# Splitting the four prompt tiles and the sample of a hybrid layer into three passes over the weights instead of two

## The reference

```python
h = x + token_mixer(rmsnorm(x))     # w_in 1024 x 3080, width-3 and width-4 causal convs, SSD scan, w_out
h = h + cross_attn(rmsnorm(h))      # w_mq, 4 heads over 256 memory tokens, w_mo
h = h + peer(rmsnorm(h))            # w_pq; 8 heads x top 16 of 128 x 128 product keys
# peer, per token: 8 x 16 experts e with gates g
#   out = sum_e g_e * gelu(x . u_tab[e]) * v_tab[e]     (16384 experts, u and v rows of 1024)
```

## Time and profile before

| what | us |
|---|---|
| median of 3 runs | 1919.24 |
| lowest, highest | 1911.52, 1919.64 |
| the profiled execution | 1920.86 |
| its span | 1918.8 |
| TensorE busy, of the span | 1707.1 |
| VectorE busy | 1245.2 |
| ScalarE busy | 371.5 |
| GpSimd busy | 734.2 |

### The profile page before, as it was taken

One profiled execution on the slowest core, in us unless ns is written; L12 is line 12 of the kernel. 1 busy time (PEld: TensorE's weight loads), 2 busy tenths in 40 slices (PEclk: granted clock), 3 DMA queues, 4 the chain that ended last, 5 costly groups with the idle time before them and its releaser, 6 DMA issues. The chain is left out here.

```text
span 1918.8 us, 19965 instructions
## 1 busy us (share of the span) xinstructions
PE 1707.1 (89%) x7088; PEld 1263.9 (66%) x7088; DVE 1245.2 (65%) x2560; ACT 371.5 (19%) x914; POOL 734.2 (38%) x597
## 2 busy tenths in 40 slices
PE   6998999989659998988686999999999999999854
PEld 5887788868546776877574666666666666666321
DVE  1252211798679767998996999676555555555773
ACT  2032023102421235523452001101000000000001
POOL 0000000223024437513774555455554555545650
PEclk9999999999769998999888999999999999999977
DMA  5533433768138959967999999999999999999992
GB/s 161 182 117 110 154 110 110 262 219 308 33 121 294 342 163 341 339 221 287 336 415 377 380 394 400 398 356 399 401 399 399 389 400 398 397 390 393 405 350 88
DMA packets 238301, 563.10 MB, mean 293 GB/s; under 512 B 17068, under 2 KB 125276, under 8 KB 236156
## 3 DMA queue, kind: packets, MB, share of 16 engines
q0 software_dynamic: 82944, 302.03, 41.6%
q1 hardware_dynamic: 152956, 243.04, 35.7%
...
...
## 5 line engine op out<-in xcount | busy, mean ns | idle before, releaser
L750 POOL DMA_INDIRECT M<-in_u_tab,IDX x288 | 366.6, 1273 | 797.1 <-DVE PEER L1675 408.3
L1064 PE MATMUL PSB<-M,HST 128*128 128x512 f32 x1024 | 466.2, 601 | 51.6 <-DVE HST L1754 49.7
L757 POOL DMA_INDIRECT M<-in_v_tab,IDX x288 | 364.0, 1264 | 340.7 <-DVE X L1696 252.0
L1056 PE MATMUL PSB<-XN,M 128*128 128x256 f32 x2048 | 467.6, 382 | 6.9 <-DMA M<-in_u_blocks 5.9
L1056 PEld LDWEIGHTS PSB<-XN,M 128*128 128x128 f32 x2048 | 391.4, 192 | 105.9 <-issue 56.6
L1064 PEld LDWEIGHTS PSB<-M,HST 128*128 128x128 f32 x1024 | 196.5, 193 | 259.5 <-issue 247.0
L1675 DVE CUSTOM_DVE_ANT_0 M<-M,XN 128x1024 f32<-128x1024 f32 x288 | 350.4, 1220 | 17.8 <-DMA M<-in_u_tab,IDX 17.2
L799 PE MATMUL PSB<-M 128*128 128x256 f32 (+1 forms) x1408 | 337.8, 402 | 11.9 <-DVE M L1345 10.6
L1696 DVE SCALAR_TENSOR_TENSOR X<-M,PEER,X 128x1024 f32<-128x1024 f32 x256 | 328.0, 1281 | 5.8 <-DMA M<-in_v_tab,IDX 3.3
L799 PEld LDWEIGHTS PSB<-M 128*128 128x128 f32 x1408 | 273.3, 196 | 70.0 <-DVE M L1345 11.5
L806 PE MATMUL PSB<-M 128*128 128x256 f32 (+1 forms) x1056 | 241.9, 389 | 0.0
(11 more groups left out here) (208 smaller groups left out, 1030.9 us busy)
## 6 DMA issues: line engine op xcount, KB each, us to landing
M<-in_u_blocks SPq DMA_DIRECT2D x128, 512.0 KB
M<-in_v_tab SPq DMA_DIRECT2D x128, 512.0 KB
M<-in_w_in SPq DMA_DIRECT2D x24, 1024.0 KB
M<-in_w_pq SPq DMA_DIRECT2D x16, 1024.0 KB
gate_spill<-M ACTq DMA_DIRECT2D x16, 1024.0 KB
M<-gate_spill SPq DMA_DIRECT2D x16, 1024.0 KB
M<-in_w_out SPq DMA_DIRECT2D x8, 1024.0 KB
M<-in_w_mq SPq DMA_DIRECT2D x8, 1024.0 KB
```

Source lines behind the costliest of these rows:

```text
L750: pool.indirect_dma_start(out=UA[:, s % RR, :], out_offset=None, in_=utab, in_offset=bass.IndirectOffsetOnAxis(ap=IDX[:, n:n + 1], axis=0) ...
L757: pool.indirect_dma_start(out=VA[:, s % RR, :], out_offset=None, in_=vtab, in_offset=bass.IndirectOffsetOnAxis(ap=IDX[:, n:n + 1], axis=0) ...
L1056: last = pe.matmul(PSB[:, 4 + b % 2, 0:2 * P], UBLK[:, b % SR, c, :], XN[:, 1:3, c * P:(c + 1) * P], start=(c == 0), stop=(c == DC - 1))
L1064: last = pe.matmul(PSB[:, 2 * t + hf, :], WR[:, b % WRING, t * P:(t + 1) * P], VBLK[:, b % SR, hf * 512:(hf + 1) * 512], start=(b == 0), s ...
```

## The change

The tiles are split into three groups: tile 0, tiles 1 and 2, and tile 3 with the sample. dense(g) is called for each, with 128, 256 and 160 tokens. The memory's kv jobs all stand in the SSD of tile 0, by KV_A to KV_C. Group 1 reads K and V back for itself, group 2 reads them again with the cache's. SP loads the 32 blocks of weights a third time. The histories of the convolutions are kept from group 0 to 1 and from 1 to 2. The planner takes costs by group for in, q and pq (pe_us). It runs in two parts. Over the rest of group 0 and group 1 the extras are the routing of tile 0 and the sparse steps. Over group 2 they are the routings of tiles 1 and 2 (hot[0]) and their one-hot batches (hot[1]), with a number of sparse steps among them: SLOT_SHARE makes it a third of the count of the others (oh and gb counted half). What is left over follows with an lk behind every six (LK_EVERY), up to 19 lk; then the others, and 12 sparse steps (BEFORE_W) ahead of the loop. tt 2 is now a job like tt 1. Scores of tile 2 lie in the buffer of the one-hots, so the first oh of each tile waits until tile 2 is routed. Before the loop SP loads the first u and v blocks in the order in which the last weight buffers come free. Left out below: the same replacement of 256 by the group's width and of group 1 by the last group in the single helpers, the wait counts of K and V by group, and the buffers' sizes.

```diff
@@ -42,9 +42,11 @@
-TG = [[0, 1], [2, 3, 4]]
-ORDER = TG[0] + TG[1]
-NG = [2 * P, 2 * P + SAM]
+TG = [[0], [1, 2], [3, 4]]
+LAST = len(TG) - 1
+ORDER = TG[0] + TG[1] + TG[2]
+WG = [P, 2 * P, P]
+NG = [P, 2 * P, P + SAM]
 DENSE = [1, 2]
@@ -53,11 +55,14 @@
 def group(t):
-    return int(t in TG[1])
+    return [t in tiles for tiles in TG].index(True)
 def pos(t):
     return ORDER.index(t)
+
+
+KV_A, KV_B, KV_C = 3, 7, 11
@@ -84,7 +89,7 @@
     else:
-        s += [("turn", 0, t) for t in TG[1]]
+        s += [("turn", 0, t) for t in TG[g]]
     for b in ("gc", "v", "gb", "x0"):
@@ -94,15 +99,14 @@
     for c in range(3, 8):
-        n = int(g == 0 or c < 5)
-        s += z[:n] + [("cs", g, c)]
-        z = z[n:]
+        s += z[:int(c < 5)] + [("cs", g, c)]
+        z = z[int(c < 5):]
+    between = z
     if g == 0:
-        s += z
         between = [("kv", kv, q, mt) for kv in range(2) for q in range(4) for mt in range(2)]
-        s += soft_chain(TG[0], [between[2 * k:2 * k + 2] for k in range(8)])
-    else:
-        s += soft_chain(TG[1], [[], z[0:1], z[1:2], [], [], z[2:3], z[3:4], [], [], [], [], []]) + [("oc",)]
+    s += soft_chain(TG[g], [between[:KV_A], between[KV_A:KV_B], between[KV_B:KV_C], between[KV_C:]] if g == 0 else [[], z[0:1], z[1:2], [], [], [], [], []])
+    if g == LAST:
+        s += [("oc",)]
     s += [("o", g, q, t) for q in range(4) for t in TG[g]]
@@ -110,24 +114,21 @@
     s += [("q", g, m) for m in range(4)]
-    s += [("kt", 1, st, q) for st in range(2 * g) for q in range(4)]
+    s += [("kt", g, st, q) for st in range(g) for q in range(4)]
     s += [("q", g, m) for m in range(4, 8)]
     for i, t in enumerate(TG[g]):
         s += [("a1", t)] + ([("a2", TG[g][i - 1])] if i else [])
     s += [("a2", TG[g][-1])]
     s += [("mo", g, q, t) for q in range(4) for t in TG[g]]
     s += [("norm", 2, t) for t in TG[g]] + [("sk", g, q) for q in range(4)] + [("turn", 2, t) for t in TG[g]]
-    s += [("keep_x", DENSE[g])]
-    if g == 0:
-        s += [("norm", 0, t) for t in TG[1]]
-    early = TG[1] if g else [0]
+    s += [("keep_x", t) for t in TG[g] if t in DENSE]
+    if g < LAST:
+        s += [("norm", 0, t) for t in TG[g + 1]]
     for m in range(16):
         s += [("pq", g, m)]
         if m % 4 == 0 and m:
-            s += [("sc", t, m // 4 - 1) for t in early]
-    s += [("sc", t, 3) for t in early]
-    if g == 0:
-        s += [("sc", 1, b) for b in range(4)]
+            s += [("sc", t, m // 4 - 1) for t in TG[g]]
+    s += [("sc", t, 3) for t in TG[g]]
     return s
@@ -135,9 +136,15 @@
           "a1": 3.8, "norm": 1.2, "keep": 0.3, "rt": 1.9, "smd": 0.8, "tt": 0.6, "oh": 1.25, "d": 1.3, "v": 1.3, "final": 1.3, "add": 22.0}
-EARLY_STEPS = 5
-G0_STEPS = 2
+SLOT_SHARE = 3
+LK_EVERY, AFTER, BEFORE_W = 6, 5, 12
 LONG = ("in", "z", "o", "q", "mo", "pq")
+
+
+def pe_us(x):
+    if x[0] in ("in", "q", "pq"):
+        return (2.2, 3.9, 2.7)[x[1]]
+    return PE_US.get(x[0], 0.0)
@@ -182,7 +189,7 @@
     lead = work.index(("sc", 0, 0)) + 1
-    out, work = work[:lead], work[lead:] + dense(1)
+    out, work = work[:lead], [work[lead:] + dense(1), dense(2)]
@@ -192,57 +199,54 @@
     slots += [("add", GSTEPS - 1)]
-    step = lambda i: slots.index(("d", i, 0))
-    one, early, mid, last = step(1), step(3), step(EARLY_STEPS), step(EARLY_STEPS + G0_STEPS)
     first = [x for h in range(PH) for x in rt(0, h)] + soft(0)
-    second = [x for h in range(PH) for x in rt(1, h)] + soft(1)
-    extra = first[:4] + merged(first[4:], slots[:one]) + merged(second, slots[one:early])
-    extra += [("tt", 1)] + merged(batches(1), slots[early:mid])
-    late_slots, slots = slots[mid:last], slots[last:]
+    one = slots.index(("d", 1, 0))
+    extra = first[:4] + merged(first[4:], slots[:one]) + slots[one:]
+    hot = [x for t in DENSE for h in range(PH) for x in rt(t, h)]
+    hot = [hot[:4 * PH] + soft(1) + hot[4 * PH:] + soft(2), batches(1) + batches(2)]
     t_pe = t_dve = 0.0
-    gone, held, late, odd = set(out), [], [], 0
-    for w in work:
-        if w[0] in LONG:
-            out += held
-            t_pe += sum(PE_US["gb"] for x in held if x[0] == "gb")
-            held = []
-        while (extra or late) and w[0] in LONG and t_dve < t_pe:
-            odd += 1
-            if late and (odd % 2 or not extra):
-                out.append(late.pop(0))
-                t_dve += dve_us(out[-1])
-                continue
-            if not extra:
-                break
-            x = extra[0]
-            if x[0] == "rt" and ("sc", x[1], x[2] // 2) not in gone:
-                break
-            if x[0] == "oh" and held:
-                break
-            extra.pop(0)
-            if x[0] in ("gb", "tt"):
-                held.append(x)
-                if x[0] == "tt":
+    gone, held = set(out), []
+    for part in range(2):
+        if part == 1:
+            n_slots = (len(hot[0]) + len(hot[1]) // 2) // SLOT_SHARE
+            n_first = n_slots * len(hot[0]) // (len(hot[0]) + len(hot[1]) // 2)
+            later = extra[n_slots:]
+            extra = merged(hot[0], extra[:n_first]) + [("tt", 1), ("tt", 2)] + merged(hot[1], extra[n_first:n_slots])
+        for w in work[part]:
+            if w[0] in LONG:
+                out += held
+                t_pe += sum(PE_US["gb"] for x in held if x[0] == "gb")
+                held = []
+            while extra and w[0] in LONG and t_dve < t_pe:
+                x = extra[0]
+                if x[0] == "rt" and ("sc", x[1], x[2] // 2) not in gone:
                     break
-                continue
-            out.append(x)
-            t_dve += dve_us(x)
-        out.append(w)
-        gone.add(w)
-        t_pe += PE_US.get(w[0], 0.0)
-        t_dve = max(t_dve, t_pe - 10) + dve_us(w)
-        if w[0] == "sc" and w[1] == NP and w[2] < 3:
-            late += rt(2, 2 * w[2]) + rt(2, 2 * w[2] + 1)
+                if x[0] in ("oh", "tt") and held:
+                    break
+                extra.pop(0)
+                if x[0] in ("gb", "tt"):
+                    held.append(x)
+                    continue
+                out.append(x)
+                t_dve += dve_us(x)
+            out.append(w)
+            gone.add(w)
+            t_pe += pe_us(w)
+            t_dve = max(t_dve, t_pe - 10) + dve_us(w)
     out += held
     ahead = [("lk", b) for b in range(HRING)]
-    out += merged(merged(late, extra), ahead[:4]) + merged(rt(2, 6) + rt(2, 7), ahead[4:8]) + ahead[8:9] + soft(2)
-    out += ahead[9:10] + late_slots[:3] + [("tt", 2)]
-    g0, n = [], P // OH_TOK
-    for k in range(0, n, 2):
-        g0 += [("oh", 2, k), ("oh", 2, k + 1)] + ahead[10 + k * 13 // n:10 + (k + 2) * 13 // n] + [("gb", 2, k), ("gb", 2, k + 1)]
-    g0 += ahead[23:]
-    out += merged(g0, late_slots[3:])
+    n = len(extra) // (HRING - AFTER)
+    k = 0
+    for n, x in enumerate(extra):
+        while k < min(HRING - AFTER, n // LK_EVERY):
+            out.append(ahead[k])
+            k += 1
+        out.append(x)
+    out += ahead[k:]
+    slots = later
+    out += slots[:BEFORE_W]
+    slots = slots[BEFORE_W:]
@@ -538,11 +542,12 @@
-            first = (slice(0, 256), slice(hist, hist + 256))
-            if g == 0:
+            w = WG[g]
+            first = (slice(0, w), slice(hist, hist + w))
+            if g < LAST:
                 return [first]
-            s0 = 256 + {0: 2, 2: 4, 3: 6}[hist]
-            return [first, (slice(256, 256 + SAM), slice(s0, s0 + SAM))]
+            s0 = w + {0: 2, 2: 4, 3: 6}[hist]
+            return [first, (slice(w, w + SAM), slice(s0, s0 + SAM))]
@@ -619,6 +624,13 @@
                 if i == BLOCK_AT[("w_mq", 2 * BW, 1)]:
+                    wait_job(sp, ("o", 1, 3, TG[1][-1]))
+                    sp.wait_ge(outs, 16 * 2)
+                    sp.dma_start(KB[0], o["mk"].rearrange("l b (t p) h d -> p (l b t) (h d)", p=P)).then_inc(kb_in, 16)
+                if i == BLOCK_AT[("w_mo", BW, 1)]:
+                    wait_job(sp, ("kt", 1, 0, 3))
+                    sp.dma_start(VV[:, 0], o["mv"].rearrange("l b (t p) h d -> p (l b t) (h d)", p=P)).then_inc(vv_in, 16)
+                if i == BLOCK_AT[("w_mq", 2 * BW, LAST)]:
@@ -674,15 +686,11 @@
                 sp.dma_start(XN[q * SAM:(q + 1) * SAM, NP, :], XN[0:SAM, NP, :]).then_inc(relaid_x, 16)
-            wait_job(sp, BLOCKS[-3][2])
-            u_block(0)
-            u_block(1)
-            wait_job(sp, BLOCKS[-2][2])
-            u_block(2)
-            v_block(0)
-            wait_job(sp, BLOCKS[-1][2])
-            v_block(1)
-            v_block(2)
+            last_of = {i % NW: BLOCKS[i][2] for i in range(len(BLOCKS) - NW, len(BLOCKS))}
+            for r in sorted(range(NW), key=lambda r: SEQN[last_of[r]]):
+                wait_job(sp, last_of[r])
+                for k in (2 * r, 2 * r + 1):
+                    (u_block if k < SR else v_block)(k % SR)
             wait_drained(sp, ("sc", NP, 3))
@@ -1727,10 +1721,9 @@
```

(7 more changed lines are left out.)

114 lines of the change are left out of this document (50 added, 64 removed).

## The result

The kernel got slower: 2041.59 us (median of 4 runs, 2035.63 to 2046.04) against 1917.3 for the kernel before in the same comparison, a ratio of 1.0651 [1.0613, 1.0689], or +124 us. The direction was forecast, the size (+36) was not, and the range (to 1992) doesn't hold it. The profiled execution has a span of 2033.9 us, 115 more than before, with TensorE busy 1746.7 us (1707.1 before).

The account below looks back on a forecast made before the run. It took TensorE's queue as what everything follows before the block loop, with TensorE and DMA full in the loop. Terms 9 + 7 + 15 + 50 - 50 + 5 = +36 us gave 1955 us; range 1908 to 1992.

Parts of the forecast that it names:

- The third pass itself: Dense part: +9 us of TensorE work, +7 for weights read a third time, +50 of gaps nothing covers (30 to 70).
- the 4 us that I gave four of them: Dense part: four gb fewer under it, 20 instead of 24, give 4 us back.
- The term for the weights: Tile 0's pass: weight loads arriving late for three buffers cost 6 to 30 us over 32 blocks, taken as +7.
- its forecast: Sign for tile 0's pass: its dense work ends near 266 us.
- my 7.1 from the earlier trace: Weight loads in tile 0's pass: a 1 MB load takes 7.1 us to land beside other traffic, as K's did.
- my estimate of 4.4 us: Weight loads: by the skill page, 2.0 us plus bytes by 436 GB/s, 4.4 us and no miss.
- The steps in the pair's pass: Pair's pq: gathers make DMA the bound, 26 us over TensorE, softened by rings to 10; +15 us (0 to 30).
- The gain: Stretch behind the dense part: 139 of 185 us remain, so -50 (-65 if nothing waits, -35 if as now).
- The loop: Expert-block loop: 201 sparse steps ahead of it for 208, seven more gathers in it, +5 us (up to 9).
- My "at 1.3 us" a step: Expert-block loop: each of seven more gathers in a stretch full of DMA costs 1.3 us.
- The rivals: Whole kernel: faster, 1895 to 1910, chance 0.14; nothing to see, 1910 to 1929, 0.16; data as bound, 1980 to 2014, 0.15.
- The data-bound one: Rival: the stream of data bounds, both DMA terms at upper ends, +93 us, 1980 to 2014; chance 0.15.

Follow-up runs that it names:

- Experiment 11: Kernel before (two groups) with no sparse step ahead of the loop, all 208 in it: 2119.38 us, ratio 1.1064 to the kernel before.
- experiment 8: Changed kernel with no sparse step up to the end of the pair's pass, 54 ahead of the loop: 2157.21 us, ratio 1.1250 to the kernel before.
- experiment 3: Changed kernel with the gelu of sparse step 4 and three steps behind it moved from the pair's pass to the third: 2037.24 us, ratio 1.0600.
- experiment 4: Changed kernel loading only an eighth of each w_mq and w_pq block in the pair's pass: 2022.74 us, ratio 1.0536 to the kernel before.
- experiment 1: Changed kernel with SP's first three gate reads issued behind the u block of lk 23, not ahead of lk 20's: 2021.63 us, ratio 1.0517.
- experiment 2: Changed kernel with lk among the batches only between oh and gb, not behind every sixth extra: 2009.63 us, ratio 1.0461 to the kernel before.
- experiment 5: Changed kernel with gate reads behind lk 23's u block and lk only between oh and gb: 1986.93 us, ratio 1.0353 to the kernel before.
- 7: Changed kernel, planner reckoning 1.8 us instead of 1.3 per d or v up to the pair's end, 161 steps ahead of the loop: 2064.26 us, ratio 1.0767.
- experiment 10: Changed kernel with the edits of experiment 5 and 34 more extras in the slots, 235 steps ahead of the loop: 1978.12 us, ratio 1.0324.
- after: The changed kernel with three groups, no further edit: 2041.59 us, ratio 1.0651 to the kernel before.
- experiment 9: Changed kernel with the edits of experiment 5, 1.8 us per step up to the pair's end, and 41 steps put among the third group's extras: 1950.42 us, 1.0197.
- experiment 6: Kernel before with five lk instead of one behind the last gb and SP's gate reads behind lk 23's u block: 1917.32 us, ratio 0.9999.

## Why the prediction was right in sign and wrong in size

**The third pass itself (9 + 7 of weights + 50 of gaps): right in its sum.** Experiment 11 has no step in the dense part and experiment 8 none up to the pair's end, so they come near to the pass alone: 899.2 - 845.3 = 54 us. Experiment 8 has 20 gb under its dense part and experiment 11 has 32; at the 4 us that I gave four of them, the twelve bring it to 66, against 66 in the forecast. It is no clean price, since experiment 8 has 29 steps in its third pass. The single gaps weren't measured one by one, so that their sum fits may be luck in part. The term for the weights (7) was too high: in tile 0's pass TensorE waited once for a weight block, 2.4 us, and the pass ended 10 us before its forecast. The page has the landing of a weight block as follows (section of DMA issues: queue, count, KB each, median us from issue to landing):

```profile
M<-in_w_in SPq DMA_DIRECT2D x36, 1024.0 KB, 6.7
M<-in_w_pq SPq DMA_DIRECT2D x24, 1024.0 KB, 6.1
...
M<-in_w_out SPq DMA_DIRECT2D x12, 1024.0 KB, 5.3
M<-in_w_mq SPq DMA_DIRECT2D x12, 1024.0 KB, 7.0
```

5.3 to 7.0 us, so my 7.1 from the earlier trace rows was a little high. These medians hide two kinds: the shortest landing of a weight block is 5.1 us and the longest 29.0, and the long ones stand beside the gathers of the pair's q and pq. In experiment 11, with hardly a gather in the dense part, w_in has a median of 5.2, w_pq of 5.3 and w_mq of 5.6. The Trainium skill, DMA: Bandwidth & Descriptors, "Anatomy of one DMA", has its fit for DMAs issued from GpSimd, and these are issued from SP; my estimate of 4.4 us from it is below the shortest landing of a weight block in either run (4.7 in experiment 11).

**The steps in the pair's pass (+15): 39 measured.** Steps cost the two-pass dense part 860.8 - 845.3 = 15.5 us and the three-pass one 953.6 - 899.2 = 54.4, so the change added 39. With the 54 of the pass that makes the 93. (With equal counts of gb it is 66 for the pass and 35 for the steps, less 8 for the eight gb that left the dense part.) The step that failed is the second half of "DMA is the bound there, 26 us over TensorE; the rings ... can soften that to 10". The first half came near: pq moved 95 x 369 = 35.1 MB, as forecast, with DMA at 1.00, and 48 gathers (49 reckoned) stretched it by 31 us. Nothing was softened. TensorE runs ahead of the gathers, but it stands 18.74 us at the last scores, where ScalarE has the gelu of the steps ahead of the copy; taking the gelu out moved the lag into the next pass (experiment 3). And q, which I had left out of this term, took 12 us more with DMA at 1.04. How much of a gather's mean of 1.48 us comes from a full DMA and how much is GpSimd's own isn't separated (experiment 4).

**The gain (-50, by a stretch of 139 us): it was 211.** Of the 72 us too little:
- 21 are SP's order (experiment 1). I wrote "then the lk left over, 24 us, more than the 18 us from last gb to first expert block", and took these lk to run under the way of the gates. I had followed TensorE's queue there, not SP's, where the reads of the gates stand ahead of the lk's u blocks.
- 31 are the place of lk (experiment 2). The failed step is "TensorE 1.9 and often one lk: about 5 us, 22 of them 112". One after the other the times listed there are 8.6 us, so the 5 takes it that batches overlap and that the lk lies in TensorE's idle time, and neither was worked out. (112 and 24 are 136, too, and not 139.) The gelu of an lk stands in ScalarE's queue ahead of the scaling, so the lk lies in the batch's chain.
- The rest, 160 against 139, is a count and a clock. 48 gb were left for the stretch, not 44: I took those still held at the last pq as under the dense part; four fewer in experiment 3 went with 10 us less. And TensorE was busy 140 us even in experiment 5, where the forecast counted 123 at full clock; the clock there was 0.92.

**The loop (+5): -4.** It is as long after (849.3) as before (853), with 202 and 208 steps ahead of it. Experiments 5, 7, 8, 10 and 11 make a curve of it: 235 and 202 steps ahead 857 and 853 us, 161 ahead 928, 54 ahead 1040, and none, in the kernel before, 1117. My "at 1.3 us" a step holds as a mean on one side of a knee that lies between 161 steps and 202 (148 steps cost 190 us, 208 cost 264), though not evenly: the first 41 cost 78 us and the next 107 only 112. With more steps ahead TensorE sets the pace (busy 719.69 of 724 us in after), with far fewer the transfers do: in the loop of experiment 8 TensorE is busy 674.52 of 794 us with DMA at 1.03, and it waits 131 us for u blocks.

```profile
1095.00:1889.00 794.00, 674.52 (x2254) 444.34 (x2253) 596.00 (x1030) 47.01 (x116) 463.38 (x399) 0.93 1.03 400
```

That is also why the steps can't simply be left out of the pair's pass: some 200 are needed ahead of the loop, and of the places tried the best for them is the stretch behind the dense part, where DMA has room (experiment 9).

**The rivals.** The data-bound one (1980 to 2014) had the right sign for the pair's pass, but neither its term for the weights nor its loss in the loop came, and the measured time lies above its range too. None of the cases had a stretch behind the dense part that gets longer; I gave that term a bound of -35, "if it goes on as now", and it was +26. All three passes' faults mended as far as I found them (experiment 9), the change still loses 2% [1.0164, 1.0229]: the dense part ends 58 us later than before, and at 151 us the stretch gives back 34. No variant was faster than the kernel before.

## What to carry to other kernels

A stall that is said to be filled with other work must be followed through every queue that this work uses, its loads on SP and its last step on ScalarE too, and not through TensorE's alone; here that was 52 of the 79 us. When a planner moves side work into an earlier stage, price it by the slowest thing that each piece passes (here its gather, by DMA and GpSimd together), don't count on a ring to hide the lag, since the stage's end collects it, and look for the knee in the later loop before giving credit for what leaves it. And work that leaves a stretch shortens it only if it set the stretch's length: here 25 steps put back into it (experiment 10 against 5) didn't lengthen it.

## What the chip showed beside this

- Three reads of 1 MB of gates occupied SP's queue for 16.56 us (13.91 in experiment 6, 8.44 in the kernel before), one of them 11.0, while the median of all 16 is 0.43. The duration of their issue instructions in after, and their landing:

```profile
L679 SPq DMA_DIRECT2D M<-gate_spill x16: 377/434/11042, 1122.8 to 1883.0; - x16
...
DMA to landing us min/median/max: 12.5/16.3/20.1
```

  What makes these issues long (the size of their pieces is one candidate) was not tried. They land in 16.3 us, which is no sign of its own: the u blocks of half the size land in a median of 7.6 in the same loop, with DMA at 1.02.
- GpSimd's instruction for one gather of 128 rows lasts from 0.93 to 1.46 us in neighbouring ones of the rows above, with 0.30 us between two: 1.24 us is the shortest distance there and among all 576 of after.
